# A two-layer decoder step on one core: the next head's projections in one-bank units between the softmax steps, the rope swap by transfers in SBUF, the third token group 360 columns wide

## The reference

```python
def rmsnorm(x, g):
    return x * rsqrt(mean(x * x, -1) + EPS) * g

def rope(x, pos):                 # rotates the first 16 of each 64 columns, halves of 8
    x1, x2 = x[..., :half], x[..., half:ROT_DIM]
    return concatenate([x1 * cos - x2 * sin, x2 * cos + x1 * sin, x[..., ROT_DIM:]])

def shared_kv(h, ln_kv, w_kv, k_norm, pos):
    kv = rmsnorm(h, ln_kv) @ w_kv
    return rope(rmsnorm(k, k_norm), pos), v       # both are outputs too

def diff_attend(q, keys, values, mask, lam):
    s = where(mask, q @ keys.T * B_HD ** -0.5, min)    # two maps per head
    p = softmax(s)
    a = p[:, :, 0] - lam * p[:, :, 1]
    return a @ values

def diff_mixer(x, keys, values, ...):
    q = rope(rmsnorm(x @ w_q, q_norm), q_pos)
    o = rmsnorm(diff_attend(q, ...), subln) * (1 - lam_init)
    return o @ w_out
```

## Time and profile before

| | us |
|---|---|
| median of 3 runs (3750.36 to 3763.46) | 3755.71 |
| the profiled execution | 3742.12 |
| its span, first to last instruction | 3740.3 |
| busy: PE / DVE / ACT / POOL | 3403.3 / 1520.0 / 1073.2 / 708.3 |
| granted TensorE clock, mean share of full | 0.956 |

### The profile page before, as it was taken

The page is one execution under the profiler, slowest core; times in us unless marked ns, Lnnn a source line. Parts: engine busy times, 40 slices in busy tenths (PEclk is TensorE's granted clock), DMA queues, the critical chain, the costliest instruction groups (busy, mean ns, idle before and its releaser), DMA issues. The chain is left out here.

```text
span 3740.3 us, 60603 instructions
## 1 busy us (share of the span) xinstructions
PE 3403.3 (91%) x24063; PEld 3227.9 (86%) x24063; DVE 1520.0 (41%) x2276; ACT 1073.2 (29%) x1895; POOL 708.3 (19%) x453
## 2 busy tenths in 40 slices
PE   5888888889888999999999888889998999999998
PEld 5787778778777999999999777777878999999998
DVE  2544554454455422222224444434446522222223
ACT  2332333333332211111113444434444221111111
POOL 1202211220221321111112211111110321111110
PEclk7998999989998999999999999999999999999999
DMA  2010100101001111111111211111111111111111
GB/s 88 19 30 19 36 19 25 30 25 29 20 24 35 45 46 46 46 41 45 46 46 40 66 49 49 50 53 44 42 49 40 45 46 46 46 46 40 46 46 65
DMA packets 254695, 155.84 MB, mean 42 GB/s; under 512 B 9520, under 2 KB 251714, under 8 KB 254402
## 3 DMA queue, kind: packets, MB, share of 16 engines
q1 hardware_dynamic: 254426, 151.91, 13.8%
HBM read 133.46 MB, written 18.42 MB: 41 GB/s over the span
## 5 line engine op out<-in xcount | busy, mean ns | idle before, releaser
L212 PE MATMUL ps<-x_hi,w_hi 128*128 128x364 f32 x2880 | 691.7, 349 | 29.9 <-DVE conv_in_sample L1154 17.5
L212 PE MATMUL ps<-x_hi,w_lo 128*128 128x364 f32 x2880 | 643.4, 332 | 3.0 <-issue 3.0
L212 PE MATMUL ps<-x_lo,w_hi 128*128 128x364 f32 x2880 | 639.9, 331 | 0.4 <-issue 0.4
L212 PEld LDWEIGHTS ps<-x_hi,w_hi 128*128 128x128 f32 x2880 | 501.5, 191 | 68.3 <-issue 22.5
L212 PEld LDWEIGHTS ps<-x_hi,w_lo 128*128 128x128 f32 x2880 | 506.7, 190 | 3.2 <-issue 3.2
L202 DVE TENSOR_TENSOR w_lo<-w_raw,w_hi 128x1024 fp32r<-128x1024 f32 x200 | 302.5, 1513 | 504.7 <-ACT w_hi L198 504.6
L212 PEld LDWEIGHTS ps<-x_lo,w_hi 128*128 128x128 f32 x2880 | 505.6, 190 | 0.7 <-issue 0.7
L198 ACT ACTIVATE w_hi<-w_raw 128x1024 fp32r<-128x1024 f32 x200 | 211.7, 1059 | 811.4 <-PE ps L212 593.8
L192 POOL TENSOR_TENSOR w_raw<-w_raw,params 128x1024 f32<-128x1024 f32 x120 | 234.2, 1952 | 954.0 <-DMA w_raw<-in_w_in_a 472.1
L1607 DVE TENSOR_TENSOR acc<-ps,acc 128x1092 f32<-128x1092 f32 x128 | 165.6, 1294 | 434.2 <-PE ps L212 434.2
L212 PE MATMUL ps<-hidden_hi,w_lo 128*128 128x364 f32 x1536 | 338.2, 328 | 0.0
(11 more groups left out here) (328 smaller groups left out, 4738.1 us busy)
## 6 DMA issues: line engine op xcount, KB each, us to landing
w_raw<-in_w_up SPq DMA_DIRECT2D x64, 512.0 KB, 3.9
w_raw<-in_w_down SPq DMA_DIRECT2D x64, 512.0 KB, 3.4
w_raw<-in_w_in_a SPq DMA_DIRECT2D x32, 512.0 KB, 4.2
w_raw<-in_w_kv SPq DMA_DIRECT2D x16, 512.0 KB, 4.0
cache_pages<-in_cache_k SPq DMA_DIRECT2D x128, 64.0 KB, 1.9
cache_pages<-in_cache_v SPq DMA_DIRECT2D x128, 64.0 KB, 1.9
x_in<-in_x_prompt SPq DMA_DIRECT2D x8, 512.0 KB, 3.9
state_sample<-in_state_delta SPq DMA_DIRECT2D x8, 512.0 KB, 4.0
```

The lines of the kernel that those rows point to most:

```text
L212: mm = nc.tensor.matmul(PS[:, bank + g, 0:GRP], wt, x[:, k, g * GRP:(g + 1) * GRP], start=(k == 0 and t == 0), stop=(k == chunks - 1 and t ...
```

## The change

**Widths.** `WIDTH` is 364, 364, 360: the third group's matmuls leave out the four padding columns, in all slabs. DVE zeroes two PSUM strips at the start; some ACT operations end at column 1088.

**Order.** Head 0's projections stay in front of the loop (`att_first_head_tensor`). For the other heads they are cut into nine units of one slab, one group, one bank (`unit_products`, 24 matmuls) and put between the softmax steps of the head before: K0, K1 in step 1, K2, Q0 in step 2, Q1 in step 3, Q2 in step 4 (two halves), V0 in steps 6 and 7 (two halves), V1 in three pieces at the end, V2 at the head of the next head's body around its key-page transposes. Banks 5 and 7 hold them; `out_sum` moves to bank 6, page transposes to banks 4 and 5. Square sums (`kq_sum`) go one by one, in bank 7, each behind the factor step of the one before. DVE takes each unit out alone. There are two pairs of k and q buffers (`KS`), even and odd heads.

**Swap.** `kq_swaps` and DVE's sine products are gone. SP issues four transfers of 8 rows x 1088 inside SBUF per k and per q (`swap`), after `b_nm` (the norm applied), and POOL does three operations instead of two (`rope`: sine, cosine, sum).

**Constants.** In head 0, `constants()` on DVE, with one memset more, comes ahead of the `lo_slab` of the second slab.

The core of the diff:

```diff
+WIDTH = [GRP, GRP, T - 2 * GRP]
...
-            cos[r], sin[r] = np.cos(ang), np.sin(ang)
+            cos[r], sin[r] = np.cos(ang), np.sin(ang) * (2 * half - 1)
...
@@ slab_products @@
-                    mm = nc.tensor.matmul(PS[:, bank + g, 0:GRP], wt, x[:, k, g * GRP:(g + 1) * GRP],
+                    mm = nc.tensor.matmul(PS[:, bank + g, 0:WIDTH[g]], wt, x[:, k, g * GRP:g * GRP + WIDTH[g]],
...
-        def body(j, a, last):
+        def key_pages(h, before=None):
+            head = ds(h, 1)
+            for n in range(NB * NPG):
+                src = cache_k[page(n), :, head, :, :].rearrange("a t b m d -> (a t b) (m d)")
+                if n == 0 and before is not None:
+                    sp.wait_ge(b_pv.sem, b_pv.at(before, SAMPLE_AT + 1))
+                sp.dma_start(CP[:, n, :], src).then_inc(b_kin, 16)
+        def swap(a, i):
+            s = i[1]
+            i = 2 * i[0] + s
+            sp.wait_ge(b_nm.sem, b_nm.at(i))
+            for m in range(2):
+                one, two = (slice(m * B_HD + c * ROT // 2, m * B_HD + (c + 1) * ROT // 2) for c in range(2))
+                sp.dma_start(SWP[one, :], KS[a][s][two, 0:T]).then_inc(b_dx, 16)
+                sp.dma_start(SWP[two, :], KS[a][s][one, 0:T]).then_inc(b_dx, 16)
...
+            swap(1 - a, (h + 1, 0))
...
+            swap(1 - a, (h + 1, 1))
+            key_pages(h + 1, before=h)
...
-    def kq_swaps(pe, s, i):
...
+    def unit_products(s, bank, g, ks):
+        for k in ks:
+            for t, (w, x) in enumerate(((WH, XH), (WH, XL), (WL, XH))):
+                mm = nc.tensor.matmul(PS[:, bank, 0:WIDTH[g]], w[s.slot][:, k, :], x[:, k, g * GRP:g * GRP + WIDTH[g]],
+                                      start=(k == 0 and t == 0), stop=(k == KC - 1 and t == 2))
+        return mm
...
@@ att_tensor, body @@
+            if not first:
+                out_sum(pe, h - 1, NT - 1)
+                pe.wait_ge(w_lo.sem, w_lo.at(v.n))
+                pe.wait_ge(b_ex.sem, b_ex.at(h, 0))
+                unit_products(v, 3, 2, range(0, 3))
+            cache_keys(0)
+            cache_keys(1)
+            if not first:
+                values(pe, h - 1, NT)
+                unit_products(v, 3, 2, range(3, 5))
...
+            scores(pe, h, a, 1)
+            pe.wait_ge(w_lo.sem, w_lo.at(k.n))
+            unit_products(k, 7, 0, range(KC)).then_inc(b_un.sem, 1)
+            probs_transpose(pe, h, 0)
+            unit_products(k, 5, 1, range(KC)).then_inc(b_un.sem, 1)
...
+            scores(pe, h, a, 5)
+            pe.wait_ge(b_ln.sem, b_ln.at(2 * h + 2, 3))
+            kq_sum(pe, h + 1, 1, 0, 7)
+            out_sum(pe, h, 2)
+            pe.wait_ge(b_ev.sem, b_ev.at(h + 1, 6))
+            probs_transpose(pe, h, 4)
+            pe.wait_ge(b_ln.sem, b_ln.at(2 * h + 3, 1))
+            kq_sum(pe, h + 1, 1, 1, 7)
+            values(pe, h, 3)
+            scores(pe, h, a, 6)
+            pe.wait_ge(b_ln.sem, b_ln.at(2 * h + 3, 2))
+            kq_sum(pe, h + 1, 1, 2, 7)
+            out_sum(pe, h, 3)
+            probs_transpose(pe, h, 5)
+            pe.wait_ge(w_lo.sem, w_lo.at(v.n))
+            pe.wait_ge(b_ln.sem, b_ln.at(2 * h + 3, 3))
+            unit_products(v, 7, 0, range(0, 4))
+            values(pe, h, 4)
+            scores(pe, h, a, 7)
+            unit_products(v, 7, 0, range(4, KC)).then_inc(b_un.sem, 1)
+            out_sum(pe, h, 4)
+            values(pe, h, SAMPLE_AT)
...
 @@ att_scalar, body, step 5 @@
+            exps(5)
+            att_ln(act, h + 1, 1, 0, 7)
+            att_out_rstd(act, h, 2)
+            probs_t(4)
+            att_square(act, n, h + 1, 1, 2)
+            att_ln(act, h + 1, 1, 1, 7)
+            hi_slab(act, att_slab(j, a + 1, 2))
+            att_out(act, h, 3)
+            exps(6)
+            att_ln(act, h + 1, 1, 2, 7)
...
 @@ att_vector, body @@
+                    elif i == 4:
+                        normed(n, h + 1, 0)
...
+                    elif i == 4:
+                        lo_slab(dve, att_slab(j, a + 1, 2))
+                    elif i == 6:
+                        normed(n, h + 1, 1)
+                        lo_slab(dve, att_slab(j, a + 2, 0))
...
 @@ att_gpsimd @@
+        def rope(a, h, s):
+            pool.wait_ge(b_dx, 64 * (i + 1))
+            nc.gpsimd.tensor_tensor(SWP[:, :], SWP[:, :], SIN[:, 0:T], ALU.mult).then_inc(b_rp.sem, 1)
+            nc.gpsimd.tensor_tensor(t, t, COS[:, 0:T], ALU.mult).then_inc(b_rp.sem, 1)
+            pool.wait_ge(b_rp.sem, b_rp.at(i, 2))
+            nc.gpsimd.tensor_tensor(t, t, SWP[:, :], ALU.add).then_inc(b_rp.sem, 1)
```

More of the change, by code:

```diff
@@ L1968, in body, with cache_keys @@
+            first, last = is_head(j, a, 0), is_head(j, a, H - 1)
+            K = KS[a][0]
+            v = att_slab(j, a, 2)
+            def cache_keys(r):
+                if r == 0:
+                    pe.wait_ge(b_kin, 16 * NB * NPG * (h + 1))
+                    pe.wait_ge(b_tc.sem, b_tc.at(h, 0))
                 if r >= 2:
@@ new lines, in att_scalar, with body, cache_keys @@
+        for s in range(2):
+            for g in range(3):
+                att_square(act, 0, 0, s, g)
+                if g >= 1:
+                    att_ln(act, 0, s, g - 1, 6 + (g - 1) % 2)
+            att_ln(act, 0, s, 2, 6)
+            att_rstd(act, 0, s)
+            hi_slab(act, att_slab(0, 0, 2) if s == 0 else att_slab(0, 1, 0))
+        def body(j, a):
+            h = 2 * j + a
+            first, last = is_head(j, a, 0), is_head(j, a, H - 1)
+            def cache_keys(r):
+                if r == 0:
+                    act.wait_ge(b_tt.sem, b_tt.at(h, 0))
@@ new lines, in att_vector, with body @@
+        dve.wait_ge(b_rs.sem, b_rs.at(0))
+        for s in range(3):
+            dve.wait_ge(w_used.sem, w_used.at(att_slab(0, 0, s).n))
+            for g in range(3):
+                unit_out(0, s, g, 3 * (s % 2) + g)
+            if s == 0:
+                constants()
+                lo_slab(dve, att_slab(0, 0, 1))
+            if s < 2:
+                normed(0, 0, s)
+                lo_slab(dve, att_slab(0, 0, 2) if s == 0 else att_slab(0, 1, 0))
+        def body(j, a):
+            h = 2 * j + a
+            first, last = is_head(j, a, 0), is_head(j, a, H - 1)
+            Q = KS[a][1]
+            if not first:
+                mix(h - 1, NT - 1)
+                dve.wait_ge(w_used.sem, w_used.at(att_slab(j, a, 2).n))
+                unit_out(a, 2, 2, 3)
@@ L2231, in body @@
                     maxima(i + 1)
-                    combine(i + 1)
-                for p in outputs_of_step(i):
-                    if p > 1:
-                        mix(p - 2)
-            for p in range(NT - 2, NT + 1):
-                mix(p)
+                if not last:
+                    if i == 0:
+                        unit(0, 0, 0, 7)
+                    elif i == 1:
+                        last_unit(0, 7)
+                    elif i == 2:
+                        unit(3, 1, 1, 5)
+                    elif i == 4:
+                        normed(n, h + 1, 0)
+                    elif i == 6:
+                        unit(4, 2, 0, 7)
@@ new lines, in body @@
+                if i + 1 < NT:
+                    combine(i + 1)
+                if i >= 2:
+                    mix(h, i - 2)
+                if not last:
+                    if i == 0:
+                        lo_slab(dve, att_slab(j, a + 1, 1))
+                        unit(1, 0, 1, 5)
+                    elif i == 1:
+                        unit(2, 1, 0, 5)
+                    elif i == 3:
+                        last_unit(1, 5)
+                    elif i == 4:
+                        lo_slab(dve, att_slab(j, a + 1, 2))
+                    elif i == 6:
+                        normed(n, h + 1, 1)
+                        lo_slab(dve, att_slab(j, a + 2, 0))
+                    elif i == 7:
+                        unit(5, 2, 1, 7)
```

603 lines of the change are left out of this document (355 added, 248 removed).

## The result

The changed kernel takes 3827.7 us (median of 4 runs, 3821.3 to 3834.1) against 3755.0: ratio **1.019** (95% interval 1.016 to 1.022), 73 us slower. The range ended at 3806, so the time did move the way that was forecast, and by far more. The profiled execution took 3833.6 us, its span 3831.8. A second profile of the same kernel, run later among the experiments, has a span of 3810.8 and the same ratio, 1.019 (1.016 to 1.022).

A forecast was written before the change was run, and what follows sets the result against it. PE was taken to bound the projections and a PE, DVE, ACT, PE chain the softmax steps; attention ending 28 us later, less 8 for widths, gave +19 to +20, so 3775 us from 3755.7; range 3743 to 3806.

The forecast's parts named there:

- Widths: Third group's 4800 matmuls, 4 columns narrower: 1.8 ns saved each if pitch goes by columns, 8 us; nothing if a floor.
- (a): Each head, page transposes to first scores: 20 us, including V2 unit 4.0 and cold start 2.4.
- (d): SP's transfers after the normed q: four swap transfers 1.9, sixteen pages 18.0, landing 1.9; sum 21.8 us.
- (b): Each head, first scores to scores of step 5: six units 24, three square sums 2, PE's own work 7.4; 33.4 us.
- (c): Each head, scores of step 5 to the next head's normed q: 27.4 us, with PE waits of 1.8 and 3.7.
- The loop: One head, (a) to (d) summed: 102.6 us against 100.3, PE standing 10 to 12 us before the key pages.
- Head 7, "as before, 48.1": Last head: 20 us to first scores, then 48.1 as before to the output projection, at 2878, 28 us later.
- Head 0: First head: second slab 6.7 us late, page transposes at 2091, q's late rope adds 6.8, first scores at 2111.5.
- The sum: Whole kernel: attention ends 28 us later, less 8 for the widths, +19 to +20 us, so 3775.
- POOL in DVE's way: Rival: k's rope on POOL delays V's lo_slab 2.5 us, seven times, +18; total +37, 3793; chance 0.20.
- Dense PE wins: Rival: ACT keeps up in steps 5 and 6, loop 94.7 us, total about -36, 3720; chance 0.16.
- What would show it: Signs: right if page transposes wait 60 to 90 us in seven times, loop 101 to 104; wrong if loop under 99.

The follow-up runs named there:

- the version with late pages: All repairs together, but the key pages sent behind q's swap again, sample output left in step 5: ratio 1.004 to the kernel before.
- the run with bank 7: Changed kernel with the last head's output sums back in bank 7 and values not waiting for the previous tile's logarithm: ratio 1.011 to the kernel before.
- the order mended: Changed kernel with all repairs together (bank 7, logarithms and norms earlier, sample output and key pages earlier, head 0's second slab first): 0.981, 3676 us.
- the order alone: Changed kernel with logarithms and norms ahead of exponentials and maxima in steps 5 to 7, output's sum ahead of V0's rest: ratio 1.011 to the kernel before.
- the pages alone: Changed kernel with sample output in step 5 instead of 7 and key pages sent behind k's swap, not q's: ratio 1.005 to the kernel before.

## Why the prediction was wrong, by its own steps

- **Widths: right.** 1.8 ns a matmul, as the pitch by columns has it. 5 us were measured for the 8 forecast, inside the interval.
- **(a) 20 us: 17.6** (2538.41 to 2555.97). The cold start was right: PE was at half clock from 2538.41 to 2543.33, which cost 2.3 us of the 2.4 forecast. The V2 unit was charged in full, 4.0, but its first nine matmuls stand ahead of the page transposes and are charged in (d) as well; the other 15 took 2.6.
- **(b) 33.4: 35.1** (2555.97 to 2591.11). The stretch is dense, as forecast. Some 1.5 us of the excess are the first dozen matmuls of K0, 0.30 us apart instead of 0.166, at a granted clock of 0.52.
- **(c) 27.4 to the normed q: 30.4.** q's swap was issued at 2621.57, when the norm had just ended. Scores 6 began at 8.9, not 7.0 (the forecast's own terms, 5.2 + 0.5 + 0.7 + 0.9, give 7.3). The maxima of step 6 began at 11.4, not 10.1, because they waited 1.3 us for those scores. V0 began at 15.5, not 14.2, and the maxima of step 7, where the forecast has scores 7 done, at 22.5, not 19.4. From there to the normed q it took 8.0 us, as forecast. Two things are missing in the step. The first q logarithm waits for DVE to have used k's factor, since both lie in `kq_rstd` (0.6 us of ACT). And `values` and the scores ran at 1.2 GHz (granted clock 0.54) behind the wait of 2.9 us: `values` took 1.9 us where 0.9 was set. Behind the wait of 2.4 us the next `values` ran at that level too, 2.3 us where 1.2 was set.
- **(d) 21.8: 23.7.** Pages 17.9 and landing 1.6 as forecast. The four transfers took 2.7 us, not 1.9, at 0.62 to 0.65 each in place of a plain one's 0.43. Between the last of them and the first page lie 1.5 us that the forecast does not have. They are not a wait for the sample output: in the version with late pages that output had ended 20 us earlier (2579.7), and the gap is the same:

```profile
2599.66 0.62 SPq L1806 DMA_DIRECT2D kq_swapped<-q_odd  x1
2601.85 17.78 SPq L1797 DMA_DIRECT2D cache_pages<-in_cache_k  x16
```

  It is 1.3 to 1.6 us in all heads of both. SP reads the first page's number from SBUF there, which is likely what it pays for; no run takes that away.
- **The loop: 102.6 forecast, 106.8 in this head, 106.3 on average.** The wait for the key pages is there and in the right place, but at 7.4 us (51.6 in seven, below the 60 to 90 named as a sign), not 10 to 12: PE came to it later (47 us behind scores 5, not 37 to 39), not the pages sooner. Six loops cost 22 us more than forecast.
- **Head 7, "as before, 48.1": this is where the mechanism failed, as against a size.** It stood for 68 with (a), and measured 86. The edit list had `out_sum` in bank 6, but the forecast took no wait from it. The wait that a shared bank adds puts each `values` behind a logarithm behind the next exponentials: 18 us, and the run with bank 7 takes 21 away (64.9). The same wait is in every other head, where it shows in step 7.
- **Head 0: +8.** The second slab came 6.8 us late, as forecast (10.86 against 4.05 of waiting). q's rope cost 10.6, not 6.8 (the other 4 to 5 us of the 8 are those of the loop): DVE's norm of q took 2.87 instead of 1.35 and its first copy 1.86 instead of 0.18, each beside a POOL operation.
- **The sum.** 18 + 22 + 8 are the 48 us by which attention missed its 28 (38 in the second profile). Another 16 of the profiled execution are the mixer's, 10 of which vanished in the second profile. So the range was missed by a step left out (the last head) and by the steps (c) and (d) and head 0 sized too small, not by the widths.
- **Rivals.** *POOL in DVE's way* happened in another place and at no cost there: V's `lo_slab` took 1.22 us, undisturbed, and the combination of step 6 was hit (0.68 us in the last head, where POOL does nothing):

```profile
2606.52 2.81 DVE L2443 TENSOR_SCALAR probs<-probs,softmax_scalars 128x896 f32<-128x896 f32 x1
2609.37 2.67 DVE L2445 SCALAR_TENSOR_TENSOR probs<-probs,softmax_scalars 128x896 f32<-128x896 f32 x1
```

```profile
2606.32 2.53 POOL L2520 TENSOR_TENSOR k_odd<-k_odd,kq_swapped 128x1088 f32<-128x1088 f32 x1
2608.81 2.28 POOL L183 TENSOR_TENSOR w_raw<-w_raw,params 128x1024 f32<-128x1024 f32 x1
```

  Scores 7 came behind it anyway (DVE waited 1.3 us for them). *Dense PE wins* fell with this order of ACT and SP, but not with the units: with the order mended the loop went to 87 us. What decides is less the amount of work than its order in the queues of ACT, DVE and SP.
- **"What would show it"** said that waits on ACT in steps 1 to 4 would break the mechanism. There were none; they stood in steps 5 and 6, where 1.8 and 3.7 us were forecast, and in step 7, where the forecast has short ones.

## What to carry to other kernels

When work is put between the steps of a chain, follow every buffer and bank that changes its user: each new sharer adds a wait, and its price is what stands ahead of the releasing instruction in that engine's queue, not the instruction itself. Short operations that others wait for go ahead of those that wait long; and transfers that free no one go behind those that someone waits for. Two closed loops of nearly the same length hide each other: here the order alone gave 31 us and the pages alone (with the sample output moved ahead) 53, while with the other one in place they gave 71 and 87. No run takes back the units between the steps or the swap by transfers, so what these bring by themselves is not known. A repair that "only moves the wait" can be worth keeping until the other is made.
